# The block inverse of the gated delta rule: one orientation updated by products, the other by transposes

## The reference, cut to what matters

```python
a_mat = jnp.where(strict, jnp.einsum('bhncd,bhnmd->bhncm', kb, k) * decay, 0.0)
rhs = jnp.concatenate([v * beta[..., None], kb * jnp.exp(g)[..., None]], axis=-1)
sol = lax.linalg.triangular_solve(a_mat + jnp.eye(c, dtype=f32), rhs,
                                  left_side=True, lower=True, unit_diagonal=True)
u, w = sol[..., :dv], sol[..., dv:]
```

## Time and profile before

| | |
|---|---|
| median of three runs | 2234.33 us (2234.1 to 2235.07) |
| the profiled execution | 2229.25 us, of which its span 2227.4 us |
| TensorE busy | 1974.4 us (89%) |
| VectorE busy | 754.7 us (34%) |
| ScalarE busy | 495.4 us (22%) |
| GpSimd busy | 158.7 us (7%) |
| mean granted TensorE clock | 0.931 of full speed |

### The profile page before, as it was taken

The page is one execution under the profiler, slowest core; times in us unless marked ns, Lnnn a source line. Parts: engine busy times, 40 slices in busy tenths (PEclk is TensorE's granted clock), DMA queues, the critical chain, the costliest instruction groups (busy, mean ns, idle before and its releaser), DMA issues.

```text
span 2227.4 us, 26152 instructions
## 1 busy us (share of the span) xinstructions
PE 1974.4 (89%) x9378; PEld 1139.9 (51%) x9379; DVE 754.7 (34%) x1568; ACT 495.4 (22%) x940; POOL 158.7 (7%) x96
## 2 busy tenths in 40 slices
PE   8989779999896669889989987899989988669997
PEld 7858644444573344343444535444458588444443
DVE  3435533233304442123322113233334255323324
ACT  1733201112203111011221101112225533111121
POOL 1110030000200030000020002000030100110000
PEclk9999979999896879889999997899999999889999
DMA  9330027999931138338994324679973300249994
GB/s 349 114 113 20 1 95 289 425 425 427 318 132 69 53 131 365 154 140 365 426 341 169 129 114 181 265 327 427 426 278 118 148 1 20 76 183 389 424 428 199
DMA packets 80016, 504.05 MB, mean 226 GB/s; under 512 B 7171, under 2 KB 11444, under 8 KB 55100
## 3 DMA queue, kind: packets, MB, share of 16 engines
q1 hardware_dynamic: 69808, 488.65, 54.5%
q0 software_dynamic: 2304, 8.39, 1.1%
q10 hardware_dynamic: 7820, 5.84, 0.9%
HBM read 501.80 MB, written 1.06 MB: 226 GB/s over the span
## 4 chain that ended last, share of the span: by engine, by line
PE 85%; DVE 10%; issue 3%; ACT 2%; DMA 1%; DVEq 0%; ACTq 0%; SPq 0%
PE bank L1687 22%; PE bank L1705 11%; PE bank L1409 10%; PE bank L1415 9%; PE bank L1678 7%; PE bank L1803 5%; PE bank L1435 4%; PE bank L1652 2%; PE bank L1517 1%; PE bank L1508 1%; PE bank L1751 1%; PE bank L1400 1%; PE bank L1698 1%; PE bank L1661 1%; PE bank L1522 1%
## 5 line engine op out<-in xcount | busy, mean ns | idle before, releaser
L1687 PE MATMUL bank<-ring,work 128*64 128x512 f32 x2176 | 485.7, 604 | 15.6 <-DVE work L1247 9.5
L1687 PEld LDWEIGHTS bank<-ring,work 128*64 128x64 f32 x2176 | 156.3, 139 | 336.1 <-issue 329.3
L1705 PE MATMUL bank<-ring,work 128*64 128x512 f32 x1088 | 242.3, 596 | 9.5 <-issue 4.9
L1409 PE MATMUL bank<-HT,ring 128*128 128x256 f32 x1024 | 232.9, 388 | 4.2 <-DMA ring<-in_a_w_in 2.3
L1409 PEld LDWEIGHTS bank<-HT,ring 128*128 128x128 f32 x1024 | 199.2, 195 | 42.4 <-issue 12.8
L1415 PE MATMUL bank<-ring,HT 128*128 128x512 f32 x448 | 193.3, 593 | 0.9 <-DVE HT L876 0.9
L1274 DVE TENSOR_TENSOR work<-bank,work 64x512 f32<-64x512 f32 x64 | 68.2, 1066 | 363.0 <-ACT work L808 363.0
L1678 PE MATMUL bank<-work 128*128 128x128 f32 x1152 | 156.4, 292 | 10.6 <-DVE work L1252 6.7
L1678 PEld LDWEIGHTS bank<-work 128*128 128x128 f32 x1152 | 143.1, 202 | 39.6 <-issue 30.3
L808 ACT ACTIVATE work<-bank 64x512 f32<-64x512 f32 x64 | 37.7, 589 | 520.9 <-PE bank L1687 520.9
L1242 DVE TENSOR_TENSOR work<-bank,lncols 128x512 f32<-128x512 f32 x72 | 49.8, 691 | 301.3 <-PE bank L1678 301.3
(11 more groups left out here) (283 smaller groups left out, 1995.9 us busy)
## 6 DMA issues: line engine op xcount, KB each, us to landing
ring<-in_e_w SPq DMA_DIRECT2D x192, 2048.0 KB, 13.0
ring<-in_a_w_in SPq DMA_DIRECT2D x16, 2048.0 KB, 16.1
ring<-in_c_w_in SPq DMA_DIRECT2D x8, 2048.0 KB, 14.8
ring<-in_b_w_in SPq DMA_DIRECT2D x6, 2048.0 KB, 17.0
ring<-in_a_w_out SPq DMA_DIRECT2D x4, 2048.0 KB, 7.8
ring<-in_c_w_out SPq DMA_DIRECT2D x4, 2048.0 KB, 7.8
ring<-in_b_w_out SPq DMA_DIRECT2D x2, 2048.0 KB, 8.8
gB<-in_ln_mix_g POOLq DMA_DIRECT2D x4, 512.0 KB, 3.9
```

Of the source, the lines that this page charges most:

```text
L1409: ins = mm(dst[:, 0:SEQ], wt[:, k, n * P:(n + 1) * P], HT[:, k, :], start=k == 0, stop=k == KC - 1)
L1687: ins = mm(bank[b][lo:lo + CAP, :], x[:, k, :], wt[:, k, :], start=k == 0, stop=k == KC - 1, skip_group_check=True)
L1705: ins = mm(bank[b][nh * CAP:(nh + 1) * CAP, :], h[:, m, :], w2[:, m, nh * 512:(nh + 1) * 512], start=m == 0, stop=m == 3, skip_group_check ...
```

## The change

Only one of the two orientations is carried by products now. In levels 1 to 4 that is `T`: it gets Ti^T Y (turn "R") subtracted. `Ti` is no longer updated in these levels; at levels 2 to 5, `Ti` is made anew by transposing `T`, four transposes per half (turn "XT"), which TensorE issues right behind `Y` of that half, and which ScalarE copies into `Ti` right behind its copy of `Y`. At level 1 `Ti` is still the one from the start. In level 5 the product is Y^T Ti, subtracted from `Ti`, as before. Both products of a level now share the turn "R" on banks 2 and 3; "XT" takes banks 4 and 5. Per half the product groups of the update go from nine to five, the subtractions on VectorE from nine to five, the transpose groups from none to four, and the copies on ScalarE from five to nine.

```diff
--- before.py
+++ after.py
@@ -131,10 +131,10 @@
                 for lv in range(1, LEVELS):
                     for hg in range(2):
                         turns.take(hg, "Y", i, tt, lv, hg)
-                    for hg in range(2):
-                        turns.take(2 + hg, "TT", i, tt, lv, hg)
-                        if lv < LEVELS - 1:
-                            turns.take(4 + hg, "T", i, tt, lv, hg)
+                        if lv > 1:
+                            turns.take(4 + hg, "XT", i, tt, lv, hg)
+                    for hg in range(2):
+                        turns.take(2 + hg, "R", i, tt, lv, hg)
                 for hg in range(2):
                     turns.take(6 + hg, "W", i, tt, hg)
                 for c in range(2):
@@ -723,11 +723,14 @@
                             if lv == 1:
                                 act.wait_ge(qdec, 4 * j + 2 * tt + hg + 1)
                             else:
-                                wait_data(act, "T", i, tt, lv - 1, hg)
+                                wait_data(act, "R", i, tt, lv - 1, hg)
                             emptied(a(Y[:, 4 * hg:4 * hg + 4, :], ps[:, :].rearrange("p (a b) -> p a b", a=4), ACT.Copy), "Y", i, tt, lv, hg)
-
-                    for hg in range(2):
-                        wait_data(act, "TT", i, tt, LEVELS - 1, hg)
+                            if lv > 1:
+                                ps = wait_data(act, "XT", i, tt, lv, hg)
+                                emptied(a(Ti[:, 4 * hg:4 * hg + 4, :], ps[:, :].rearrange("p (a b) -> p a b", a=4), ACT.Copy), "XT", i, tt, lv, hg)
+
+                    for hg in range(2):
+                        wait_data(act, "R", i, tt, LEVELS - 1, hg)
                         for h in range(4 * hg, 4 * hg + 4):
                             ins = a(kG[:, h, :], Ktok[:, h, :], ACT.Copy, scale=gsc[:, 4, tt, h:h + 1])
                         ins.then_inc(kscaled, 1)
@@ -1050,15 +1053,11 @@
                             mask(lv + 1)
                         for hg in range(2):
                             hs = slice(4 * hg, 4 * hg + 4)
-                            psT = wait_data(dve, "TT", i, tt, lv, hg)
-                            if lv < LEVELS - 1:
-                                psU = wait_data(dve, "T", i, tt, lv, hg)
+                            ps = wait_data(dve, "R", i, tt, lv, hg)
                             if lv > 1:
-                                wait_copy(dve, "TT", i, tt, lv - 1, hg)
-                                wait_copy(dve, "T", i, tt, lv - 1, hg)
-                            emptied(v.tensor_tensor(Ti[:, hs, :], Ti[:, hs, :], psT[:, :].rearrange("p (a b) -> p a b", a=4), ALU.subtract), "TT", i, tt, lv, hg)
-                            if lv < LEVELS - 1:
-                                emptied(v.tensor_tensor(T[:, hs, :], T[:, hs, :], psU[:, :].rearrange("p (a b) -> p a b", a=4), ALU.subtract), "T", i, tt, lv, hg)
+                                wait_copy(dve, "R", i, tt, lv - 1, hg)
+                            dst = T if lv < LEVELS - 1 else Ti
+                            emptied(v.tensor_tensor(dst[:, hs, :], dst[:, hs, :], ps[:, :].rearrange("p (a b) -> p a b", a=4), ALU.subtract), "R", i, tt, lv, hg)
                     for c in range(2):
                         r0 = slice(64 * c, 64 * c + 64)
                         last = (tt, c) == (TT - 1, 1)
@@ -1503,28 +1502,29 @@
 
                             ps = fill("Y", i, tt, lv, hg)
                             pe.wait_ge(masked, 20 * j + 10 * tt + 2 * (lv - 1) + hg + 1)
-                            wait_copy(pe, "T0", i, tt, hg) if lv == 1 else wait_copy(pe, "T", i, tt, lv - 1, hg)
+                            wait_copy(pe, "T0", i, tt, hg) if lv == 1 else wait_copy(pe, "R", i, tt, lv - 1, hg)
                             for h in range(4 * hg, 4 * hg + 4):
                                 ins = mm(ps[:, (h % 4) * P:(h % 4 + 1) * P], AM[:, h, :], T[:, h, :], start=True, stop=True)
                             done(ins, "Y", i, tt, lv, hg)
+                            if lv > 1:
+                                ps = fill("XT", i, tt, lv, hg)
+                                for h in range(4 * hg, 4 * hg + 4):
+                                    ins = tr(ps[:, (h % 4) * P:(h % 4 + 1) * P], T[:, h, :], ident)
+                                done(ins, "XT", i, tt, lv, hg)
                         for hg in range(2):
 
                             wait_copy(pe, "Y", i, tt, lv, hg)
                             if lv > 1:
-                                wait_copy(pe, "TT", i, tt, lv - 1, hg)
-                            ps = fill("TT", i, tt, lv, hg)
+                                wait_copy(pe, "XT", i, tt, lv, hg)
+                            ps = fill("R", i, tt, lv, hg)
                             for h in range(4 * hg, 4 * hg + 4):
-                                ins = mm(ps[:, (h % 4) * P:(h % 4 + 1) * P], Y[:, h, :], Ti[:, h, :], start=True, stop=True)
-                            done(ins, "TT", i, tt, lv, hg)
-                            if lv < LEVELS - 1:
-                                ps = fill("T", i, tt, lv, hg)
-                                for h in range(4 * hg, 4 * hg + 4):
-                                    ins = mm(ps[:, (h % 4) * P:(h % 4 + 1) * P], Ti[:, h, :], Y[:, h, :], start=True, stop=True)
-                                done(ins, "T", i, tt, lv, hg)
+                                left, right = (Ti, Y) if lv < LEVELS - 1 else (Y, Ti)
+                                ins = mm(ps[:, (h % 4) * P:(h % 4 + 1) * P], left[:, h, :], right[:, h, :], start=True, stop=True)
+                            done(ins, "R", i, tt, lv, hg)
                     for hg in range(2):
                         ps = fill("W", i, tt, hg)
                         pe.wait_ge(kscaled, 4 * j + 2 * tt + hg + 1)
-                        wait_copy(pe, "TT", i, tt, LEVELS - 1, hg)
+                        wait_copy(pe, "R", i, tt, LEVELS - 1, hg)
                         for h in range(4 * hg, 4 * hg + 4):
                             ins = mm(ps[:, (h % 4) * P:(h % 4 + 1) * P], kG[:, h, :], Ti[:, h, :], start=True, stop=True)
                         done(ins, "W", i, tt, hg)
```

## The result

The changed kernel took 2214.53 us (median of 4 runs, 2210.45 to 2215.78), the kernel before in the same comparison 2234.22 (4 runs, 2228.72 to 2235.07). The ratio is 0.9914 with a 95% interval of 0.9898 to 0.9929: 19 us off, 16 to 23. The profiled execution took 2210.45 us, its span 2208.6, against 2229.25 and 2227.4 before.

A forecast was written before the change was run, and what follows sets the result against it. TensorE's order, closed by VectorE's second subtraction, was taken to bound each 6.25 us pass. At 4.80 us, 1.45 less, 16 passes save 23.2 us: from the median 2234.33 to 2211.1 us, range 2204 to 2221.

The forecast's parts named there:

- The bound: Inverse levels: TensorE's order, closed by VectorE's second subtraction, from `T`, sets the pass of 6.25 us.
- Steps 1 and 2: Levels 1 to 4: removed product and subtraction cut the 0.65 us bubble to 0.1-0.2; with `Y` and XT, pass 4.74-4.84 us.
- the 0.1 for two switches: Levels, TensorE: switching from transposes to products may cost 0.05 us, twice per pass, giving 4.84 in place of 4.74.
- Step 3: Levels, ScalarE: added copies fit with 0.4 us of cover; R of half 1 up to 0.2 us late, absorbed.
- Rival 2: Levels: ScalarE's copies set the pass at about 5.1 us; 18 us saved in all, 2216 us; chance 8%.
- Steps 4 and 5: Levels, level 5 and after: VectorE's masks stay hidden; ScalarE's scaling starts as before, `W` moves with R; no added cost.
- The transposes and the clock: Levels: transposes count towards full clock, as in the trace at 273-276 us, against the skill's rule; clock stays 1.00.
- Rival 1: Levels: transposes leave TensorE too quiet, clock falls to 0.50, pass about 9.2 us; +47 us, 2281 us; chance 4%.
- What survives: Whole kernel: everything behind the blocks just comes earlier, so the 23.2 us survive, plus or minus 4 us for the clock.
- rival 3: Behind the blocks and in the experts: low-clock places grow by 5 to 15 us, 2216 to 2226 us; chance 8%.

The follow-up runs named there:

- dummies: Products of the identity added where TensorE waits behind the mixers: on the changed kernel 2198.8 us (0.9849), on the kernel before 2228.21 us (0.9985).
- the first pair: The first profiles of the changed kernel and the kernel before, no further edit: profiled executions 2210.45 against 2229.25 us.

## Why the prediction was right, point by point

- **The bound.** Right. The 6.25 us were TensorE's order closed by VectorE's second subtraction: turning that order round gave 5.42 with nothing removed.
- **Steps 1 and 2.** Right, but for a slip of 0.01 in the sum (2.0 + 2.73 is 4.73). R to `Y` is 1.93 us (2.0 forecast), then 0.96, 0.44, 0.89, 0.44 in the timeline, each as worked out. The switch from transposes to products costs nothing: 165.63 to 166.07 is 0.44. That is the mis-sized term: without the 0.1 for two switches, and with 1.93 for 2.0, the pass is 4.66 and not 4.80, and 16 passes bring 25.3 us where I had 23.2.
- **Step 3.** Right. ScalarE's four copies fit, two in a row start 0.50 us apart; R of half 1 starts 0.05 us late, and its second record 0.07 more, which costs nothing here because `Y` waits for VectorE until then. Taking the transposes away and doubling them moved the pass by 0.81 and 0.88, so TensorE set it. Rival 2 did not occur.
- **Steps 4 and 5.** Right; the masks and the scaling moved along, `W` waits 0.39 us for the scaling as it waited 0.46.
- **The transposes and the clock.** Rival 1 did not occur, and with twice the transposes the clock was 1.00 still.
- **What survives.** Here the forecast was off: I had all of it coming through, plus or minus 4. The whole got 18 to 20 us in two comparisons. That the 2211.1 stands so close to the measured 2214.53 is partly luck, because two errors oppose each other: 2 us more in the blocks, 5 to 7 less outside. That is rival 3 in its size, which had 8%. My argument against it, that there is no reason for one sign, is what failed: ten runs of the changed kernel have a lower clock than fifty of the one before. Shown is that the low time is longer in the mean, that the stage behind a mixer takes 2.3 us more when the clock comes back late, that this happened in none of six stages of the kernel before and its variants and in eleven of fourteen of the changed one and its variants, and that with dummies in both kernels, at one mean clock, the gap between them opens to 29 us. Not shown is why the change makes the late return the common case in these stages; the attempt to undo it by a delay repaired the stage and not the whole.
- **The gaps in the experts' first pass.** These the forecast did not have. Of the 4.6 us that the experts of layer 0 lost in the first pair, 2.9 are such gaps and 1.3 the L1678 at half clock. In layer 0 the gaps of over 0.4 us add 2.1 to 4.1 us in the five profiles of kernels with the changed kernel's count of TensorE records (9250) and 3.5 in the kernel before with dummies, and 0 or 0.4 in the seven others. Each kernel has such gaps in later layers too, so the sum over all layers differs less: 10.6 us in both profiles of the kernel before without dummies or another order, 10.2 to 13.8 in the four of the changed kernel with and without a delay. The page has a DMA queue named `instruction` with 58 packets of 16 KB. All 76 such gaps of the thirteen traces lie 23 to 41 us behind the first gather of their layer and end 1.2 to 2.1 us after a packet of this queue has ended; of all moments in that stretch only 16% lie so. That speaks for a wait for the program's own code, at a time when the expert weights fill the DMA engines (share 1.01 from 346.6 to 360 us in the changed kernel), and would explain why each kernel has the gaps in other places. No run moved the code, so it is not shown.

## What to carry to other kernels

Where one engine's order is closed by another's last instruction, look first which of the two results the next step needs and make that one first: here this alone was worth half of what the loop gained. Then the cheaper operation counts in full, because the loop is bound by the engine that runs it; price the loop once per engine and check the others' cover. A gain of 1% from such a loop is known to the hundredth in the timeline, and to a fifth of itself in the whole, since the clock outside the loop differs from kernel to kernel and from run to run. Before naming a place that gave time back, compare how long TensorE works at half clock, stage by stage: the mean clock was the same in pairs of profiles that differed here.

## What the runs showed of the hardware

- A group of four float32 transposes of 128x128 takes 0.44 us of TensorE at 1.00, half of the eight records of four products (0.89), and mixing the two costs nothing.
- With transposes in 32% of TensorE's time (products in 64%) the granted clock stayed at 1.00 through the levels. The trace before had the clock back at the end of sixteen transposes and nothing else; in the changed kernel the same sixteen behind block 4 did not bring it back: it came back 9.2 to 9.3 us after their start, behind 4.5 us of products. The rule of the Trainium skill ("TensorE: Matmul & The Clock Gate", "Part 4: PE-mode transpose") that full clock does not engage in transpose mode would fit the second of these; the levels, at 1.00 with a third of the time in transposes, show only that they don't pull a warm clock down.
- 40, 34 and 25 idle products in TensorE's waits were worth 13 us to one kernel and 2 to 3 us to the other at the same mean clock of 0.953. Two differences in the profiles are of that size, and no run tests them: the stages behind the two mixers got 9.6 us shorter in the changed kernel (142.4 to 132.8 in sum) and 5.8 in the kernel before (137.9 to 132.1), and the gaps in the experts' first passes grew by 1 us in the first and by 4 us in the second.
- Executions of one kernel spread over 5 to 17 us on this single core, and in the kernel before the mean granted clock follows that spread. The stage that varies most is the experts of layer 1, 336 to 345 us, with 36 to 54 us of it at half clock.
- In the first pass of the experts TensorE stops up to three times per layer, for 0.4 to 3.0 us, each time until 1.2 to 2.1 us after a packet of the instruction queue.
